# A hybrid decoder trunk on one core: the order of the norms, of their evacuations, of the output projection's tiles and of the router's ranking

## The reference

```
for l in range(2):
    h = rmsnorm(x, attn_norm[l])
    proj = h @ w_in[l]                      # 1024 x 2832, feeds the four mixers
    mix = concat(oa, ob, oc, od)            # 256 x 1024
    x = x + mix @ w_out[l]
    h = rmsnorm(x, ffn_norm[l])
    x = x + (swiglu(h, ...) if l == 0 else moe_swiglu(h, ...))
return rmsnorm(x, final_norm)

def moe_swiglu(h, router, w1, w3, w2):
    top_vals, top_idx = lax.top_k(h @ router, 2)        # 2 of 8 experts
    gates = softmax(top_vals)
    out = sum over e of combine[..., e] * swiglu(h, w1[e], w3[e], w2[e])
```

## Time and profile before

| | us |
|---|---|
| median of 3 runs | 948.43 (947.99 to 950.49) |
| the profiled execution | 948.73 |
| its span in the trace | 946.9 |
| PE busy in the span | 926.2 (98%) |
| DVE, POOL, ACT busy | 425.0, 215.6, 181.2 |

### The profile page before, as it was taken

One profiled execution on the slowest core, in us unless ns is written; L12 is line 12 of the kernel. 1 busy time (PEld: TensorE's weight loads), 2 busy tenths in 40 slices (PEclk: granted clock), 3 DMA queues, 4 the chain that ended last, 5 costly groups with the idle time before them and its releaser, 6 DMA issues.

```text
span 946.9 us, 30492 instructions
## 1 busy us (share of the span) xinstructions
PE 926.2 (98%) x13688; PEld 741.7 (78%) x13688; DVE 425.0 (45%) x871; ACT 181.2 (19%) x416; POOL 215.6 (23%) x213
## 2 busy tenths in 40 slices
PE   8999999999999999999999999999999999999996
PEld 7897875699999644799787569686969696969692
DVE  4854666587666545795376442212121303030204
ACT  3354141211111000314525020000000101010102
POOL 3820632133333433572072100010101000000000
PEclk9999999999999999999999989999999999999999
DMA  9843201555555545454310898999999999999931
GB/s 318 278 151 118 91 2 46 170 167 169 169 168 169 210 172 172 139 172 137 103 51 2 299 374 315 339 381 400 398 400 387 413 386 414 385 411 388 396 128 44
DMA packets 90122, 223.30 MB, mean 236 GB/s; under 512 B 6080, under 2 KB 53952, under 8 KB 89920
## 3 DMA queue, kind: packets, MB, share of 16 engines
q1 hardware_dynamic: 86528, 212.29, 60.8%
q0 software_dynamic: 1680, 5.90, 2.6%
q10 hardware_dynamic: 1840, 4.00, 1.3%
HBM read 215.89 MB, written 6.29 MB: 235 GB/s over the span
## 4 chain that ended last, share of the span: by engine, by line
PE 94%; DVE 2%; ACT 2%; issue 1%; DMA 0%; POOL 0%; DVEq 0%; POOLq 0%; ACTq 0%
PE bank L683 92%; DVE x_sb L1988 1%; PE bank L1412 1%; DVE tok L2017 0%; PE bank L694 0%; ACT arena L1719 0%; DVE hT L1988 0%; DMA x_sb<-in_x 0%; ACT tok L1554 0%; PE bank L724 0%; PE bank L1138 0%; ACT arena L1716 0%; DVE tok L1988 0%; ACT arena L1568 0%; POOL small L1808 0%
## 5 line engine op out<-in xcount | busy, mean ns | idle before, releaser
L683 PE MATMUL bank<-arena 128*64 128x96 f32 (+6 forms) x8592 | 504.1, 276 | 4.6 <-issue 2.3
L683 PEld LDWEIGHTS bank<-arena 128*64 128x64 f32 (+4 forms) x8592 | 380.1, 136 | 126.7 <-issue 104.6
L1988 DVE TENSOR_TENSOR arena<-arena 128x512 f32<-128x512 f32 (+3 forms) x139 | 129.8, 948 | 33.5 <-PE bank L683 22.4
L683 PE MATMUL bank<-arena,hT 128*128 128x256 f32 (+4 forms) x588 | 126.7, 386 | 0.2
L683 PE MATMUL bank<-hT,arena 128*64 128x128 f32 (+2 forms) x1596 | 116.2, 285 | 2.6 <-DVE hT L1988 2.6
L1988 DVE TENSOR_TENSOR arena<-arena,bank 128x128 f32<-128x128 f32 (+3 forms) x159 | 57.4, 386 | 132.3 <-ACT arena L1782 105.6
L683 PEld LDWEIGHTS bank<-hT,arena 128*64 128x64 f32 (+2 forms) x1596 | 104.4, 141 | 11.4 <-issue 5.0
L683 PEld LDWEIGHTS bank<-arena,hT 128*128 128x128 f32 (+2 forms) x588 | 81.8, 173 | 35.1 <-issue 26.8
L683 PE MATMUL bank<-tok,arena 128*64 128x128 f32 x1824 | 104.9, 273 | 0.0
L683 PEld LDWEIGHTS bank<-tok,arena 128*64 128x64 f32 x1824 | 100.7, 137 | 0.0
L1967 POOL DMA_INDIRECT x_rows<-arena,rows_out x7 | 10.1, 1447 | 210.2 <-DVE arena L2627 210.2
(11 more groups left out here) (224 smaller groups left out, 673.1 us busy)
## 6 DMA issues: line engine op xcount, KB each, us to landing
arena<-in_moe_w SPq DMA_DIRECT2D x128, 704.0 KB, 11.8
arena<-in_moe_w SPq DMA_DIRECT2D x40, 1024.0 KB, 9.5
arena<-in_ffn_w SPq DMA_DIRECT2D x33, 1024.0 KB, 5.5
arena<-in_w_in SPq DMA_DIRECT2D x22, 1024.0 KB, 6.2
arena<-in_w_out SPq DMA_DIRECT2D x8, 1024.0 KB, 4.9
arena<-in_moe_w SPq DMA_DIRECT2D x8, 512.0 KB, 13.2
arena<-in_w_in SPq DMA_DIRECT2D x2, 1088.0 KB, 5.5
consts<-in_consts SPq DMA_DIRECT2D x1, 1330.5 KB, 6.2
```

Of the source, the lines that this page charges most:

```text
L683: return nc.tensor.matmul(o, lhsT, rhs, start=start, stop=stop, skip_group_check=True)
L1988: return v.tensor_tensor(o, a, b, op)
```

## The change

Three parts, and small edits that go with them.

1. **Opening.** `norm_rows` puts the mean of tile 1 and its request between the two halves of tile 0's scaling. ACT evacuates both banks of tile 0, DVE both of tile 1. The first projection P0 is no longer one pass over 256 tokens: `project_first` multiplies the first four feature chunks for tile 0 (as halves of 64 columns), then for tile 1 (128 columns), and then the last four chunks for both.
2. **Output projection and the second norm.** After the transposed fourth mixer the parts run as 0:(2), 3:(0, 1), 0:(3), 3:(2), where before they ran as 0:(3), 3:(0, 1, 2, 3); then come the transposes of tile 0 (F0, F1), and the last part 3:(3) behind them. DVE evacuates F0 ahead of `add_bank(3)`, ACT evacuates F1 ahead of the last square. One more quarter product (layer 0) or router product (layer 1) stands ahead of tile 1's transposes.
3. **Router.** The two rounds of "largest, first of the equal, mask" are replaced by ranks: every logit is compared with all eight, once for greater and once for equal and earlier, the sums are ranks, and rank < 2 is chosen. The softmax takes its sum over the chosen. The filler steps go from 14, 6 and 4 to 6, 2 and 2. Bank G1 is evacuated by DVE in one operation and not in four.

```
+                  ("iota", CAP), ("token", NT), ("spare", 1), ("earlier", N_EXPERTS * N_EXPERTS)):
...
+            def project_first(name, l, n, features):
+                wait_piece(pe, n)
+                wait_open(pe, name, l)
+                w = ring[:, slot(n), 0:KC * pieces[n][3]].rearrange("p (c n) -> p c n", c=KC)
+                for t in range(NT):
+                    wait_evacuated(pe, features[2 * t], l)
+                    product = mm if t else mm_halves
+                    for j in range(2):
+                        for k in range(4):
+                            product(bank(name, l)[:, j * SEQ + t * P:j * SEQ + (t + 1) * P], w[:, k, j * P:(j + 1) * P],
+                                    hT[:, k, t * P:(t + 1) * P], start=(t == 0 and j == 0 and k == 0))
+                for t in range(NT):
+                    wait_evacuated(pe, features[2 * t + 1], l)
+                for j in range(2):
+                    for k in range(4, KC):
+                        last = mm(bank(name, l)[:, j * SEQ:(j + 1) * SEQ], w[:, k, j * P:(j + 1) * P], hT[:, k, :],
+                                  stop=(k == KC - 1))
+                fills(last, name, l)
...
-                w_out_products(l, 0, (0, 1, 2))
+                w_out_products(l, 0, (0, 1))
                 pe.wait_ge(sem("mix_ready"), NT * (l + 1))
                 mix_to_features(3, l)
+                w_out_products(l, 0, (2,))
+                w_out_products(l, 3, (0, 1))
                 w_out_products(l, 0, (3,))
-                w_out_products(l, 3, (0, 1, 2, 3))
+                w_out_products(l, 3, (2,))
+                tile_to_features(("F0", "F1", "F2", "F3"), l, 1, 0)
+                w_out_products(l, 3, (3,))
...
-                between_blocks(14)
+                between_blocks(6)
...
-                between_blocks(6)
+                between_blocks(2)
...
-                between_blocks(4)
+                between_blocks(2)
...
             def norm_rows(names, l, gain, k):
-                for t in range(NT):
-                    half_mean(k, t)
-                    scale_rows(ask_row_scale(k, t), t)
+                half_mean(k, 0)
+                asked = ask_row_scale(k, 0)
+                scale_half_row(asked, 0, 0)
+                half_mean(k, 1)
+                asked = ask_row_scale(k, 1)
+                scale_half_row(asked - 1, 0, 1)
+                scale_rows(asked, 1)
...
                 add_bank(prefix, l, 2)
                 scale_rows(asked, 0)
+                dve.wait_ge(sem("gains_landed"), 16 * (m + 1))
+                if prefix == "O":
+                    features_out(names[0], m, gain, 0)
                 add_bank(prefix, l, 3)
...
-                first_of(lg3, best, oh)
-                link(stt(tm, oh, -3.0e38, lg3, ALU.mult, ALU.add))
-                first_of(tm, second, cb)
-                link(tt(oh, oh, cb, ALU.add))
+                tt(above, other, own, ALU.is_gt)
+                link(tt(equal, other, own, ALU.is_equal))
+                link(tt(equal, equal, earlier.unsqueeze(1).broadcast_to(shape), ALU.mult))
+                link(tt(above, above, equal, ALU.add))
+                link(v.tensor_reduce(rank, above, AX_X, ALU.add))
...
+                v.tensor_scalar(oh, rank, 2.0, None, ALU.is_lt).then_inc(sem("chosen_ready"), 1)
...
-HALVED = 12
+HALVED = 10
```

More of the change, by code:

```diff
@@ L712, in between_blocks, with tile_to_features @@
                         idle_products(1, banks[2], ident[:, 0:HALF], consts[:, 0:P])
-            def rows_to_features(names, l, which, sums=None, first=None):
-                if sums is not None:
-                    wait_evacuated(pe, *sums)
-                for t in range(NT):
[L719 to L728, removed]
+            def tile_to_features(names, l, which, t):
+                for i in range(2):
+                    name = names[2 * t + i]
+                    pe.wait_ge(sem("h_ready"), 2 * (NT * norm_index(l, which) + t) + i + 1)
+                    wait_open(pe, name, l)
+                    for c in range(4):
+                        last = nc.tensor.transpose(bank(name, l)[:, c * P:(c + 1) * P],
+                                                   tok[:, t, (4 * i + c) * P:(4 * i + c + 1) * P], ident)
+                    fills(last, name, l)
             def wait_features(names, l, k):
@@ L1293, in dense @@
             def dense(l):
-                wait_evacuated(pe, "F1", l)
-                for j in range(2):
-                    up_second(l, 0, j)
+                up_second(l, 0, 1)
                 wait_evacuated(pe, "F3", l)
@@ L1555, in square_sums, with tile_evacuation @@
                                              accum_out=ss[:, 2 * t + i:2 * t + i + 1]).then_inc(sem("squares"), 1)
[L1557 to L1562, removed]
[L1563 to L1564 removed]
+            def tile_evacuation(names, l, gain, t, i=1):
+                name = names[2 * t + i]
+                wait_full(act, name, l)
+                for c in range(4 * i, 4 * i + 4):
+                    last = nc.scalar.activation(hT[:, c, t * P:(t + 1) * P],
+                                                bank(name, l)[:, (c % 4) * P:(c % 4 + 1) * P], ACT.Copy,
+                                                scale=param(gain, c))
+                frees(last, name, l)
             def evacuate(name, l, dst, src):
@@ L1581, in layer_mixers @@
             def layer_mixers(l):
-                feature_evacuation(("T0", "T1", "T2", "T3"), l, "attn_norm")
+                for i in range(2):
+                    if l == 0:
+                        tile_evacuation(("T0", "T1", "T2", "T3"), l, "attn_norm", 0, i)
+                    else:
+                        tile_evacuation(("T0", "T1", "T2", "T3"), l, "attn_norm", i)
                 if l == 0:
@@ L2533, in gates @@
-                tt(r_s[:, 0:2], second, best, ALU.subtract).then_inc(sem("gates_shifted"), 1)
+                shape = [P, NT, N_EXPERTS, N_EXPERTS]
+                other, own = lg3.unsqueeze(2).broadcast_to(shape), lg3.unsqueeze(3).broadcast_to(shape)
+                tt(above, other, own, ALU.is_gt)
+                link(tt(equal, other, own, ALU.is_equal))
+                earlier = const("earlier").rearrange("p (e f) -> p e f", e=N_EXPERTS)
+                link(tt(equal, equal, earlier.unsqueeze(1).broadcast_to(shape), ALU.mult))
@@ L2534, in gates @@
+                dve.wait_ge(sem("chosen_ready"), 1)
+                for e8 in tables[1:]:
+                    v.tensor_copy(chosen[:, :, e8], oh)
                 wait_full(dve, "POS", l)
                 at = bank("POS", l)[:, 0:16].rearrange("p (t e) -> p t e", t=NT)
-                for q in range(MAX_PASSES + 1):
+                link(v.tensor_scalar(place[:, :, tables[0]], at, 0.0, None, ALU.add))
+                one_hot(pick, 0, chosen).then_inc(sem("picks"), 1)
+                for q in range(1, MAX_PASSES + 1):
@@ L2577, in _ @@
                     wait_full(dve, "G1", l)
-                    for c in range(4, 8):
-                        last = slots_in(c, 0)
-                    frees(last, "G1", l)
+                    at = PARAM["ffn_norm"][0] + KC // 2
+                    frees(tt(slot_h[:, KC // 2:, :], bank("G1", l)[:, 0:4 * CAP].rearrange("p (c s) -> p c s", c=4),
+                             along(params[:, at:at + KC // 2], CAP), ALU.mult), "G1", l)
                     def next_rows(at):
```

91 lines of the change are left out of this document (44 added, 47 removed).

## The result

| | before | after |
|---|---|---|
| median, 12 runs each on one chip | 949.35 us | 953.16 us (949.51 to 955.22) |
| ratio (worked out over the runs, so not quite that of the medians) | 1 | 1.0043, 95% interval 1.0032 to 1.0054 |
| profiled execution, its span | 948.73, 946.9 | 953.52, 951.7 |

The forecast was 949.5 with a range of 946.5 to 952.0. The time lies above the range, and the bound of 0.3% is passed on the slow side.

The account below looks back on a forecast made before the run. PE, holding 94% of the chain, was taken as the bound. Opening -0.5, layer 0 +1.45 and layer 1 +0.1 gave +1.05 on 948.73, 949.8; less 0.30 for the median, 949.5, range 946.5 to 952.0.

Parts of the forecast that it names:

- the bound of 0.3%: Whole kernel: 2.85 us, what a measurement can tell from no change, 945.6 to 951.3; slower given 0.18.
- Opening, -0.5: Opening: P0 starts 0.87 us earlier but grows by 0.37; net -0.5, bounds -0.9 and +0.1.
- rival A: Layer 1: clock stays low into the gather, PEclk 0.50 at its start; total +3.05, 951.5; chance 20%.
- Layer 0, +1.45: Layer 0, second norm: PE stops 1.6 us behind O2, `up_third` starts later; +1.45, bounds +0.6 and +2.0.
- Rival C: Both layers: tile 0's rows scaled under 0:(3) and 3:(2), blocks 1.65 us earlier; total -2.25, 946.2; chance 7%.
- Rival D: Layer 0 falls to the low clock once, 3.4 us of work at half rate; total +2.75, 951.2; chance 7%.
- Layer 1, transposes +2.6: Layer 1, second norm: PE waits for tile 1's rows, transposes at 559.5 for 556.89, +2.6 us.
- Layer 1, logits +2.4 and count +0.4: Layer 1 router, low clock assumed: logits at 563.8 (+2.4), place counting at 566.2 (+0.4) behind six filler steps.
- Rival B: Layer 1: clock hardly falls, logits at 562.5, counting at 564.4; total -1.2, 947.2; chance 15%.
- Ranking 1.85: Layer 1 router: logits to chosen takes 1.85 us by ranks, for 3.07 before, gain 1.2.
- a count at the lower level: Layer 1: if place counting runs at the low clock, 0.4 to 0.9 us is added.
- The upper bound of +2.1: Layer 1 sum, taken as +0.1: its upper bound, with slower counting and half the gather paid twice.

Follow-up runs that it names:

- b_open: Kernel before with the new opening alone, fillers 12, 5, 3 of 128 columns to hold the program's length; 948.85 us, ratio 0.9989.
- a_order: Changed kernel with the scaling of tile 0 ahead of the addition of O2 on DVE, both layers; 949.51 us, ratio 1.0009.
- the four kernels side by side: Low-clock time by order and filler: old/long (before) 11.4 us, old/short (a_oldw) 13.4, new/long (a_p0_fill14) 12.1, new/short (after) 17.3.
- a_new1: Changed kernel with the new output projection and second norm order in layer 1 only, old order in layer 0; 951.29 us, ratio 1.0029.
- b_narrow: Kernel before with its 36 filler products reading 4 columns, places and weights kept; 952.79 us, ratio 1.0037.
- a_oldw: Changed kernel with part 2 undone in both layers; opening, ranks and short fillers stay; 946.61 us, ratio 0.998.
- a_oldw_moved: Changed kernel, part 2 undone, filler steps moved: three ahead of tile 0's router product, two ahead of tile 1's transposes, then 3, 1, 1; 947.14 us.
- a_new0: Changed kernel with the new output projection and second norm order in layer 0 only, old order in layer 1; 946.8 us, ratio 0.9979.
- a_moved: Changed kernel, layer 1 fillers moved: three steps ahead of the router's first products, three ahead of tile 1's transposes, then 2, 1, 1; 951.40 us.
- a_p0_fill14: Changed kernel with P0 in one pass again and the fillers of before, same program length; 953.08 us, ratio 1.0042.

## Why the prediction was wrong

- **Opening, -0.5**: right. P0 at 10.21 (predicted 10.25), its bank out 0.64 earlier, b_open -0.6.
- **The starting point**: 0.9 of the 3.7 us between 949.5 and 953.16 come from the median of three runs that the forecast started from. On the median of twelve it would read 950.4, its range would end at 952.9, and rival A would read 952.4. The time would still lie above the range.
- **Layer 0, +1.45**: right, 1.5 in the trace, for the reason given: `add_bank(2)` stands in DVE's queue ahead of `scale_rows(0)`. Stops of 1.43, 0.30 and 0.20 against 1.6, 0.2 and 0.35. Rival C is refuted by the trace of after; a_order is C's premise made true, and even it ends at 949.51 and not at 946.2. Rival D did not come: PEclk stayed at 1.00 in layer 0 of after. The profiled a_order does have 3.4 us at the lower level in layer 0, from 142.04 on, but that is 35 us ahead of the output projection and not at D's stop.
- **Layer 1, transposes +2.6**: right, 560.27 for 556.89 less the 0.86 carried in, +2.5. The router's products ahead of them waited 0.87 us for DVE, which was not foreseen but cost nothing, as PE waited for tile 1's rows anyway: in the code the logits' bank is that of O3, so that `add_bank(3)` must have freed it. Before, the router stood behind that addition too.
- **Layer 1, logits +2.4 and count +0.4**: wrong, and it looks right by coincidence. The logits at 563.79 and the count at 566.32 fall on the predicted 563.8 and 566.2, but the prediction counts from the trace of before: less the 0.86 they came at +1.5 and -0.3. The clock fell 4 us later than before, so that from the transposes to the logits 3.52 us went by, where the forecast took 4.3 for the lower level. So the count came 0.7 us earlier than forecast, which hides part of the miss behind it. Rival B, a clock that hardly falls, did not come either: it fell for 13.65 us, only later.
- **Ranking 1.85**: 1.88 (565.50 + 0.17 - 563.79), and the six filler steps held PE for 2.53 us behind the logits, predicted 2.4.
- **The step that failed**: the clock's way back. The forecast's sum had 0.45 us for a count at the lower level ("0.4 to 0.9 is added") and nothing for the gather, which it left at the full clock. Measured, at PEclk 0.50: count 1.02 us longer, gather 2.31 longer, 3.3 us in place of 0.45. The upper bound of +2.1 and the price of rival A rest on half a gather at the lower level, 0.85 + 1.45 = 2.3. A further 0.96 us in the first expert's pass was in no step. Rival A's mechanism and its deciding point (PEclk 0.50 at the gather's start) came true, and both of its conditions, the thinner stretch and the shorter filler, are what the four kernels side by side show; it gave 951.5 and had 20%. The argument against it, 24 records of filler directly behind the logits, read a recovery of before (1.00 at 565 to 567) as something that filler brings at once. In after PE was busy 2.00 of 2.00 us at 565 to 567 and the level stayed until 574.75.
- **Two slips in the working**: rival A's terms, -0.35 + 0.85 + 1.45, give 1.95 and not 2.1, and rival C's 946.2 lies below the range that is said to take it in.
- **The cause, as far as shown**: part 2 costs 6.5 us. 3.65 of it (3.1 in mean spans) go with the order of two calls on DVE (a_order), and that is stops and hardly clock; 4.7 appear with the new order in layer 1 alone (a_new1). Of the 3.8 us between before and after about 2.9 are clock. b_narrow shows that a low count and gather alone are enough to lose 3.3, and the four kernels that it takes the new order and the short filler together to lengthen the low time. Why the level sometimes lasts 6.8 and sometimes 13.65 us stays open.
- **The first pass's 0.96 is not the clock's**: b_narrow, low until 573.61, has 37.30 us from the loop's start to the next pass and b_open, low until 563.90, has 38.71, where before has 37.44 and after 38.40. Some 0.6 of it goes with `project_first`, the rest lies in stops booked as "issue" and in the first 492 records (21.15 us for 20.93); what makes either stays open.
- The Trainium skill, in "TensorE: Matmul & The Clock Gate", section "What's actually happening", says that the number of slow products at a start varies between runs of one kernel, with the phase. The runs here agree in kind, though in the middle of a program and not at its start: a_oldw ran from 943.76 to 952.75 at mean clocks of 0.998 to 0.988, and its profiled run (943.96) has no low stretch in the router's stage.
- The range was cut for one low stretch of usual length. A time with the whole gather and count at 1.2 GHz, 3.3 us in place of 2.3, belonged in it.

Among the fastest versions found is the one that keeps the opening and the ranks with the short filler, and the old order of `w_out`: a_oldw, 946.61, ratio 0.998. Its interval ends at 0.9998, so the gain over before is small and only just clear of noise. a_oldw_moved (947.14, interval 0.9965 to 0.9988) is as good and varies less (945.52 to 948.04), and a_new0 (946.8, 0.9967 to 0.9991) can't be told from either.

## What to carry to other kernels

Where PE's program is reordered so that a result comes earlier, look at the queue of the engine that consumes it: one call in the wrong place there (here an addition ahead of a scaling) turned the gain into a stop. Where the granted clock falls in a stage, price all of the dense work behind it at half the clock, not a part of it, and compare many runs, since the profiled one shows one case of several. Start a forecast from as many runs as there are. When a forecast's time is held against a trace, take off first what came in from the stages ahead: here two marks looked right only because 0.86 us had been carried in. Fillers are a trade: they paid where PE stood anyway (a_moved), and were worth nothing where they held the next product back (a_p0_fill14).

## What the runs showed of the hardware that was not expected

- Thirty-two PE records more or less (13720 or 13656 for 13688) doubled the bytes of the instruction queue, 1.00 to 2.05 and 2.03 MB, and cost 56 and 81 us: PE stops for 2 us at a time with no releaser in the profile. The same long filler at 13688 records (a_p0_fill14) moved 1.00 MB and had no such stops in its later passes. In the first pass the kernels of 13688 records have such stops too, 128 records apart (0.80 and 1.53 us in before).
- PEclk stayed at 0.50 while PE was busy 2.00 of 2.00 us: in after at 565 to 567 and 571 to 573, and in b_narrow at the same places. By the clock records the low stretches in the router's stage were 3.4 us long in the profiled a_moved, 6.8 in before and 13.65 in after, b_narrow and a_new0, and a_oldw had none.
- Products of 4 columns took no less time than products of 64: 0.106 us a record in b_narrow, nearly all at the lower level, for 0.117 in after at the lower level.
